# Gated FFN: the gate products of seven of eleven rounds in Strassen pairs, on mixed forms of the normed operand

## What is computed

```python
def first_block(...):
    for i in range(DEPTH):                       # DEPTH = 2
        ...
        x = x + rms_norm(merged @ w_out[i], norm_mix_post[i])
        h = rms_norm(x, norm_ffn_pre[i])
        ff = (jax.nn.silu(h @ w_ffn_gate[i]) * (h @ w_ffn_up[i])) @ w_ffn_down[i]
        x = x + rms_norm(ff, norm_ffn_post[i])
        ...
```

## Time and profile before

| | |
|---|---|
| median of three runs | 2928.62 us |
| the profiled execution, its own time | 2927.99 us |
| its span in the trace | 2926.2 us |
| around the span | 1.8 us |
| TensorE busy | 2906.4 us, 99% of the span |
| VectorE, ScalarE, GpSimd busy | 53%, 46%, 49% |
| granted TensorE clock | 1.00 in all slices |
| HBM traffic | 93 GB/s over the span |

### The profile page before, as it was taken

The page is one execution under the profiler, slowest core; times in us unless marked ns, Lnnn a source line. Parts: engine busy times, 40 slices in busy tenths (PEclk is TensorE's granted clock), DMA queues, the critical chain, the costliest instruction groups (busy, mean ns, idle before and its releaser), DMA issues. The chain is left out here.

```text
span 2926.2 us, 40035 instructions
## 1 busy us (share of the span) xinstructions
PE 2906.4 (99%) x14888; PEld 2405.1 (82%) x14888; DVE 1545.5 (53%) x2476; ACT 1342.3 (46%) x2089; POOL 1426.2 (49%) x825
## 2 busy tenths in 40 slices
PE   9999999999999999999999999999999999999999
PEld 7888888888878888888888877778888887888888
DVE  5657534221053667434222076655767688476766
ACT  4556545232243556445222255554444447443443
POOL 4454355444444554355444444344647462456655
PEclk9999999999999999999999999999999999999999
DMA  4222232233322222233233322113323222223322
GB/s 145 74 87 80 80 122 94 93 100 101 102 93 87 73 94 66 94 116 105 94 100 101 103 85 79 59 44 101 101 94 101 94 97 92 93 94 108 102 94 101
DMA packets 77305, 273.78 MB, mean 94 GB/s; under 512 B 8776, under 2 KB 9416, under 8 KB 77152
## 3 DMA queue, kind: packets, MB, share of 16 engines
q1 hardware_dynamic: 74112, 266.05, 27.6%
q10 hardware_dynamic: 3040, 5.64, 0.6%
HBM read 269.55 MB, written 2.10 MB: 93 GB/s over the span
## 5 line engine op out<-in xcount | busy, mean ns | idle before, releaser
L3238 POOL TENSOR_TENSOR WLO<-WRAW,WHI 128x1024 fp32r<-128x1024 f32 x355 | 859.3, 2424 | 1006.3 <-ACT WHI L1704 1003.4
L934 PE MATMUL ps<-HH,WHI 128*128 128x512 f32 x2144 | 842.2, 393 | 3.1 <-POOL WLO L3238 1.3
L936 PE MATMUL ps<-HH,WLO 128*128 128x512 f32 x2144 | 834.8, 389 | 0.0
L935 PE MATMUL ps<-HL,WHI 128*128 128x512 f32 x2144 | 834.5, 389 | 0.0
L1704 ACT ACTIVATE WHI<-WRAW 128x1024 fp32r<-128x1024 f32 x435 | 457.2, 1052 | 154.2 <-DMA WRAW<-wall 154.2
L934 PEld LDWEIGHTS ps<-HH,WHI 128*128 128x128 f32 x2144 | 402.6, 188 | 92.2 <-issue 5.3
L936 PEld LDWEIGHTS ps<-HH,WLO 128*128 128x128 f32 x2144 | 402.5, 188 | 84.5
L935 PEld LDWEIGHTS ps<-HL,WHI 128*128 128x128 f32 x2144 | 402.8, 188 | 80.7
L2463 DVE TENSOR_TENSOR ACC<-ACC,SQ 128x512 f32<-128x512 f32 x78 | 70.6, 906 | 281.3 <-ACT SQ L2000 271.1
L2981 DVE SCALAR_TENSOR_TENSOR ps<-U,COLS,ps 128x512 f32<-128x512 f32 x192 | 145.1, 756 | 85.2 <-ACT ps L2174 81.8
L3348 POOL TENSOR_SCALAR SG<-SG,RS 128x512 f32<-128x512 f32 (+3 forms) x104 | 110.1, 1069 | 140.4 <-DVE RS L2743 140.4
(11 more groups left out here) (460 smaller groups left out, 5749.0 us busy)
## 6 DMA issues: line engine op xcount, KB each, us to landing
WRAW<-wall SPq DMA_DIRECT2D x502, 512.0 KB, 3.3
y<-X ACTq DMA_DIRECT2D x8, 256.0 KB, 2.1
X<-xin SPq DMA_DIRECT2D x3, 512.0 KB, 7.7
DFT<-dft ACTq DMA_DIRECT2D x4, 258.0 KB, 4.1
PT_IN<-pin ACTq DMA_DIRECT2D x2, 512.0 KB, 3.6
DIL<-dil ACTq DMA_DIRECT2D x1, 768.0 KB, 4.4
X<-xin SPq DMA_DIRECT2D x2, 256.0 KB, 4.6
COLS<-cols ACTq DMA_DIRECT2D x1, 290.5 KB, 5.3
```

The costliest lines, as they stand in the source:

```text
L934: pe.matmul(out_, WHI[w_at], x_hi, start=first, stop=False)
L935: pe.matmul(out_, WHI[w_at], x_lo, start=False, stop=False)
L936: return pe.matmul(out_, WLO[w_at], x_hi, start=False, stop=last)
L3238: pool.tensor_tensor(WLO[:, s, :], whole, WHI[:, s, :].bitcast(F32), ALU.subtract).then_inc(wt_lo, 1)
```

## The change

In each layer, the round order becomes: one round as before (gate, up, gate, up), then seven rounds of up, up and two paired gate units (`swiglu_pairs`), then three rounds as before. A paired gate unit holds 4 of the 8 blocks of two gate tiles; both units of a round give two gate tiles. The number of weight units and bytes stays the same.

```diff
-EXTRA = 4
+EXTRA, EXTRA_1 = 4, 3
+GATE_ROUNDS = 7
+KEPT_TILES = 2 + 2 * GATE_ROUNDS
...
 def summing(n):
     t, k = UNITS[n][4] // P, UNITS[n][2]
+    if t != 2 and n in GATES:
+        return {"pool": (), "vector": FORMS}
     if t == 2:
         return {"pool": FORMS, "vector": ()}
...
+            def swiglu_pairs(st):                      # TensorE
+                for r in range(GATE_ROUNDS):
+                    for j in range(2):
+                        tile(st, 4 * r + j, 2 * r + j, 0, pair["H"], DT)
+                    for b in range(2):
+                        u = st.unit(4 * r + 2 + b)
...
+                        if b == 0 and r:
+                            pe.wait_ge(S["pair_step"], st.at("pair_step", PAIR_STEPS * r))
...
+                        pe.wait_ge(slot_lo, PAIRED[u] + 1)
+                        for i, m in SLOTS_FIRST:
+                            k = 2 * b + i
+                            if r == 0 and m == 2:
+                                pe.wait_ge(S["mixed_ready"], st.at("mixed_ready", k + 1))
+                            if (i, m) == (0, 3):
+                                weights(u)
...
+            def swiglu_pairs(st):                      # ScalarE
+                mixed_hi(st, 0)
+                rows_gained(st, 2)
+                mixed_hi(st, 1)
+                rows_gained(st, 3)
+                for kp in range(2, 4):
+                    mixed_hi(st, kp)
+                for r in range(GATE_ROUNDS):
+                    for j in range(4):
+                        prepared(st, 4 * r + j)
...
+                    act.activation(TM[:, 0, 0:HALF], ps[4][:, 0:HALF], ACT.Copy).then_inc(S["first_copied"], 1)
+                    for k in range(2):
+                        act.wait_ge(S["pair_step"], st.at("pair_step", PAIR_STEPS * r + 6 + k))
+                        act.activation(SG[:, k, :], SG[:, k, :], ACT.Silu).then_inc(S["gate_ready"], 1)
...
+            def rows_mixed(st, kp):                    # VectorE
+                b, t = halves(gained(kp)), halves(mixed_at(kp))
+                dve.wait_ge(S["rows_gained"], st.at("rows_gained", kp + 1))
+                if kp >= 2:
+                    dve.wait_ge(S["mixed_ready"], st.at("mixed_ready", kp - 1))
+                dve.tensor_tensor(t[:, 0:2, :], b[:, 1:2, :].to_broadcast([P, 2, HALF]), b[:, 0:4:3, :], ALU.subtract).then_inc(S["mixed"], 1)
+                dve.wait_ge(S["mixed"], st.at("mixed", 3 * kp + 1))
+                dve.tensor_tensor(t[:, 2, :], t[:, 1, :], b[:, 0, :], ALU.subtract).then_inc(S["mixed"], 1)
+                dve.wait_ge(S["mixed"], st.at("mixed", 3 * kp + 2))
+                dve.tensor_tensor(t[:, 3, :], b[:, 2, :], t[:, 2, :], ALU.add).then_inc(S["mixed"], 1)
+
+            def rows_low(st, kp):
+                dve.wait_ge(S["mixed_hi_ready"], st.at("mixed_hi_ready", kp + 1))
+                at = slice(2 * kp, 2 * kp + 2)
+                dve.tensor_tensor(HML[:, at, :], mixed_at(kp), HMH[:, at, :].bitcast(F32), ALU.subtract).then_inc(S["mixed_ready"], 1)
...
+            def swiglu_pairs(st):
+                rows_low(st, 0)
+                rows_mixed(st, 2)
+                rows_low(st, 1)
+                rows_mixed(st, 3)
+                rows_low(st, 2)
+                rows_low(st, 3)
+                for r in range(GATE_ROUNDS):
+                    sums_of(st, 4 * r)
...
+                    sums_of(st, 4 * r + 3)
+                    gates_added(st, r)
+                    for m in range(2):
...
+                        dve.tensor_tensor(FR[:, 2 + 2 * r + m, :], SG[:, 2 + m, :], SG[:, m, :], ALU.mult).then_inc(S["product_ready"], 1)
```

```diff
                     for j in range(4):
                         k = j // 2
+                        if st.kept is not None and 4 * r + j < KEPT_TILES // 2:
+                            for t in range(8 * r + 2 * j, 8 * r + 2 * j + 2):
+                                dve.wait_ge(S["kept_hi_ready"], st.kept.at("kept_hi_ready", t + 1))
+                                dve.tensor_tensor(F1L[:, t, :], FR[:, t, :], F1H[:, t, :].bitcast(F32), ALU.subtract).then_inc(S["kept_ready"], 1)
```

```diff
-            return {3: (0, 1), 4: (), 5: (2, 3)}.get(j, tiles_done(st, j - 1))
+            return {3: (0,), 4: (), 5: (1, 2, 3)}.get(j, tiles_done(st, j - 1))
```

More of the change, by code:

```diff
@@ L172, in unit_list @@
         u.append(("w_ple_proj", l, 0, PLE, 4 * P, 4 * P))
-        for n in range(FT1):
-            product("w_ffn_gate", l, DM, n * P)
-            product("w_ffn_up", l, DM, n * P)
+        for n in range(0, FT1, 2):
+            if 2 <= n < KEPT_TILES:
+                for m in range(2):
+                    product("w_ffn_up", l, DM, (n + m) * P)
+                for b in range(2):
+                    u.append(("w_ffn_gate paired", l, 2 * b, 2, n * P, 2 * P))
+                continue
+            for m in range(2):
+                product("w_ffn_gate", l, DM, (n + m) * P)
+                product("w_ffn_up", l, DM, (n + m) * P)
         for n in range(DT):
@@ L218 @@
 PAIRED = {n: q for q, n in enumerate(n for n, unit in enumerate(UNITS) if unit[0].endswith(" paired"))}
+GATES = {n: q for n, q in PAIRED.items() if UNITS[n][0] == "w_ffn_gate paired"}
 FORMS = (R1, R3, R2, R4)
@@ L254, in __init__ @@
         self.late, self.res, self.late_copy = False, res, None
+        self.pairs, self.kept = None, None
         self.tables, self.halves, self.begun, self.cq, self.op_hi = None, False, False, None, 0
@@ L867, in sums_free, with extras, gained, mixed_at @@
         def sums_free(engine, n):
-            if PAIRED[n] >= EXTRA:
-                engine.wait_ge(unit_used, PAIRED_UNITS[PAIRED[n] - EXTRA] + 1)
+            if extra_before(n) is not None:
+                engine.wait_ge(unit_used, extra_before(n) + 1)
+        def extras(n):
+            e = extra_slot(n)
+            return tuple(x[:, e, :] for x in ((XRAW1, XLO1, XHI1) if n in GATES else (XRAW, XLO, XHI)))
+        def gained(kp):
+            return SG[:, 2:4, :] if kp % 2 == 0 else HG1[:, :, :]
+        def mixed_at(kp):
+            return SQ[:, :, :] if kp % 2 == 0 else HT1[:, :, :]
         def sums_ready(engine, n):
@@ L1298, in out_y @@
                 n = st.units // 4
+                if st.kept is not None:
+                    pe.wait_ge(S["kept_ready"], st.kept.at("kept_ready", KEPT_TILES))
                 def body(r):
@@ L2022, in residual, with prepared, rows_gained, mixed_hi @@
                 repeat(act, st, body, 0 if st.u0 + st.reps * st.units + AHEAD < NU and not st.halves else st.reps)
+            def prepared(st, j, r=0):
+                n = st.unit(j, r) + AHEAD
+                if n in PAIRED:
+                    split_kept(n)
+                    split_sums(n)
+                else:
+                    split_of(st, j, r)
+            def rows_gained(st, kp):
+                if kp >= 2:
+                    act.wait_ge(S["mixed"], st.at("mixed", 3 * (kp - 2) + 3))
+                x = gained(kp)
+                for m in range(2):
+                    ins = act.activation(x[:, m, :], X[:, 2 * kp + m, :], ACT.Copy, scale=col(st.made.gain, 2 * kp + m))
+                ins.then_inc(S["rows_gained"], 1)
+            def mixed_hi(st, kp):
+                act.wait_ge(S["mixed"], st.at("mixed", 3 * kp + 3))
+                act.activation(HMH[:, 2 * kp:2 * kp + 2, :], mixed_at(kp), ACT.Copy).then_inc(S["mixed_hi_ready"], 1)
             def swiglu(st):
                 def body(r):
-                    first = isinstance(r, int) and r == 0
+                    first = r == 0 and st.norm is not None
                     if first:
@@ L2795, in body @@
                             scaled(st, j, r, SG[:, k, :])
+                            if st.pairs is not None and j == 2:
+                                rows_mixed(st.pairs, 0)
+                                rows_mixed(st.pairs, 1)
                             continue
@@ L2799, in body @@
                         dve.wait_ge(S["gate_ready"], st.at("gate_ready", 1 + k, r))
+                        if st.pairs is not None:
+                            dve.tensor_tensor(FR[:, k, :], TM[:, k, :], SG[:, k, :], ALU.mult).then_inc(S["product_ready"], 1)
+                            continue
                         dve.tensor_tensor(TM[:, k, :], TM[:, k, :], SG[:, k, :], ALU.mult).then_inc(S["product_ready"], 1)
-                        remainder(st, (tile_of(r * 2 + k, F1H), tile_of(r * 2 + k, F1L)), TM[:, k, :], 1 + k, r)
@@ L2802, in swiglu @@
-                repeat(dve, st, body)
+                        t = st.t + r * 2 + k
+                        remainder(st, (F1H[:, t, :], F1L[:, t, :]), TM[:, k, :], 1 + k, r)
+                if st.pairs is not None:
+                    sums_of(st, 3)
+            def swiglu_pairs(st):
[7 more added lines that the diff above has]
+                    sums_of(st, 4 * r)
+                    for m in range(2):
+                        dve.wait_ge(unit_used, st.unit(4 * r + m) + 1)
+                        if r:
```

(10 more changed lines are left out.)

123 lines of the change are left out of this document (97 added, 26 removed).

## The result

The changed kernel takes **2943.78 us**, the median of five runs (2942.81 to 2945.25); the kernel before, run beside it, 2928.74. The ratio is 1.0049 (1.0035 to 1.0062): 15.0 us slower. The forecast was 2935.3 us and its range ended at 2941.5, so the direction it leaned to was right and the size was not even in the range. One run of an experiment (e8) took 3196.37 us at a mean granted clock of 0.85, where all others stand at 0.99 or more, and is left out of its median.

A forecast was written before the change was run, and what follows sets the result against it. TensorE was taken as the bound, busy 2906 of 2926 us. 2927.99 - 11.2 (pairs) + 17.9 (first paired rounds) = 2934.7, and 0.6 for the runs' median gives 2935.3 us; range 2920.5 to 2941.5.

The forecast's parts named there:

- A small edit: Last down stage: finishing tile 1 later, behind the second pair's adds, costs 0, between -0.9 and +0.9 us.
- The 16 kept tiles are split: End of the gated stage: splitting two kept tiles per product tile, 2 x 0.69 us on VectorE, costs nothing.
- signs of being wrong: Wrong if mixing steps stand at 0.43 us, a TensorE wait returns each round, or TensorE waits in the kept tiles' split.
- I cost rounds 2 to 7 at nothing: Full paired rounds of 21.0 us: operands come with 2.8 us to spare, so no TensorE wait.
- Full rounds are late too: Rival: 0.5 us lost in each of 12 full paired rounds adds 6 us, giving 2941; chance 0.10.
- The first paired round: Mixing held up by GpSimd's lock makes TensorE wait 8.55 us in layer 0, 9.35 in layer 1: +17.9 us.
- the lock hardly binds: Rival: first paired rounds lose only 3.6 us together, net -7.6, giving 2921.0 us; chance 0.20.
- half of it: Rival: the second mixing group slips through before GpSimd's slot remainder; 13.2 us lost, net +2.0, 2930.6 us; chance 0.20.
- What the pairs take off: Gated stages: each of 28 paired units saves 0.40 us of TensorE's matmul time, -11.2 us.

The follow-up runs named there:

- e8: Changed kernel with 14 matmuls of 512 columns added on TensorE ahead of the wait for the norm's sum of squares behind the last `down`: 2939.97 us.
- e1: Changed kernel with tile 1's finish in the last down stage put back ahead of the second pair's adds: 2938.13 us.
- e2: Kernel before with only tile 1's finish moved behind the second pair's adds: 2932.42 us against 2927.58.
- e3: Changed kernel with 28 and 7 extra matmuls of 256 columns ahead of the first paired round's waits for mixed groups 0 and 1: 2942.06 us.
- e4: Changed kernel with ScalarE rounding the next two kept tiles ahead of the next unit's weights, not behind them: 2938.80 us.
- e5: Changed kernel with GpSimd's six operations cut to 16 columns for each of the first two paired units of each layer: 2926.29 us.
- e10: e3 with ScalarE rounding the second paired unit ahead of the fourth mixed group, not behind it: 2949.87 us.
- e15: e12 with the next tile's weights also rounded ahead of the fourth mixed group, and four paired rounds per layer, not six: 2924.02 us.
- e13: Changed kernel with the edits of e1 and e4 together: 2934.82 us, +5.9 to the kernel before.
- e12: Changed kernel with e1 and e4, two plain and six paired rounds, mixing gathered, second plain round's last tile's weights rounded before the third mixed group: 2921.34 us.

## Why the prediction was wrong

**"A small edit ... 0, between -0.9 and +0.9."** This step failed: 4.5 to 4.8 us (e1, e2). I saw the two locked operations and their 5.2 us, and reasoned that moving them was neutral, "TensorE would meet the norm's sum of squares earlier by as much as it gained". But the norm's sum is the end of a chain of squares and sums on VectorE; behind the first pair's adds tile 1's finish fell on GpSimd's back-to-back remainders just as before, pushed tile 3's into the next ones, and so delayed the second pair's adds by 3.1 us, for which no cover was left. I priced what TensorE would gain (0.92 us, and it did) and never walked VectorE's chain to its end.

**The clock.** The prediction takes full clock for granted everywhere and prices no fall of it. It is 3.2 us of the step above by the medians and 3.3 by the traces (e8). In the first paired rounds, where the trace shows more half clock, it is nothing (e3), so the timetable didn't suffer. That was luck: at half clock the first unit ended 0.7 us before the second unit's remainder came.

**"The 16 kept tiles are split ... nothing."** The second step that failed: 4.4 us (e4; 2.0 in each layer's stage). I summed busy time (2 x 0.69 beside 2.1 us in each 5.44) with the free length, and one paragraph further on showed from the earlier trace rows that such operations take 2.4 to 2.9 us beside GpSimd. Two a tile took 3.1, which with the 2.1 of own work and the handovers to ScalarE is more than 5.44. I also named a TensorE wait in this place among the signs of being wrong, and it was there.

**"I cost rounds 2 to 7 at nothing."** Right: 130.00 of 130.00 us busy from 510 to 640, no wait. *Full rounds are late too* is dead.

**"The first paired round," +17.9.** Right: 17.5 by e5. Groups 0 and 1 and the second unit came within 0.7 us of the timetable. The rivals *the lock hardly binds* and *half of it* are dead; e10 shows the hold-up with nothing else changed.

**"What the pairs take off," -11.2.** Right: 0.39 us a unit (e15).

So the kernel of the forecast's terms exists: e13, +5.9 for +6.7. The whole miss is in the two lines that were costed at nothing, 4.5 and 4.4 us, the second by the very rule that the first paired round was priced with.

What stays open: how the 5 us of tile 1's finish part between wait and clock in the kernel before. e8 parts them in the changed kernel alone; against the kernel before, e2's trace loses 2.1 us from 2300 to the start of the second pair's adds, and 2.9 more by 2400, at half clock, but no run feeds TensorE there. e10's 7.8 us are not parted either.

## What to carry to other kernels

An edit that "costs nothing" needs the same walk as the main term: free lengths are not to be used for VectorE operations on two SBUF operands that can meet a GpSimd instruction, and which of two engines starts first is often the order of two lines on a third one. A pair scheme has an entrance fee, paid where operand, weights and sums are all new; it pays to buy one more plain round and hide the fee there (24 units with waits of 1.3 and 1.6 us, e12, stand at -7.6; 28 that pay the fee, e13, at +5.9), and in that round ScalarE must round weights as they land. Half clock in a trace is a cost only where no wait stands behind it: look for the next wait before pricing it.
